# A streaming encoder step: two of eight modulation vectors computed ahead of the SSD, six during the QKV projection, and QKV with weights stationary in chunks of 512 tokens

## The chip, the cores and the metric

One core of one Trainium2 chip. The metric is the device time of one execution in microseconds (us). The core's engines are TensorE (PE, with its weight loads shown apart as PEld), VectorE (DVE), ScalarE (ACT), GpSimd (POOL) and SyncE (SP), which here only issues DMAs. Each engine runs its own instructions in order; semaphores tie them together.

## What is computed

One layer of a hybrid encoder for two request groups: 2048 prompt tokens and 64 sample tokens, model width 1024. The parts that matter here:

```
mod = (silu(c) @ w_ada + b_ada)[:, None, :]              # w_ada (1024, 6144), c: one row per group
sh1, sc1, g1, sh2, sc2, g2 = split(mod, 6)
h = rmsnorm(x, norm1_w) * (1 + sc1) + sh1
m, states = mixer(h, ...)
x = x + g1 * m
h = rmsnorm(x, norm2_w) * (1 + sc2) + sh2
x = x + g2 * hier_moe(h)
...
# mixer:
proj = h @ w_in                                          # w_in (1024, 2832)
z, xbc, dt_raw = proj[..., :i0], proj[..., i0:i1], proj[..., i1:i2]
q, k, v, f_raw = ...                                     # q, k, v: 512 columns each
... conv, SSD scan (Mamba-2) over xbc, dt; forgetting attention over q, k, v, cumsum(log_sigmoid(f_raw + f_bias))
... concatenated @ w_out
# after the layer:
sh_f, sc_f = split(silu(c) @ w_ada_f + b_ada_f, 2)       # w_ada_f (1024, 2048)
y = rmsnorm(y, final_norm_w) * (1 + sc_f) + sh_f
```

The first two modulation vectors (sh1, sc1) are needed by the first norm, the other six only from the output projection on. k and v are returned as well, for both groups.

## The kernel before

All arithmetic is float32. The large products are made of three products of rounded halves (`product3`, lines 265 to 269: high times high, and the two cross terms, of type fp32r); a weight is split by ACT (rounded copy, L255) and DVE (the rest, L260). Small products (modulation, parts of the SSD) are plain float32 matmuls, which the trace shows as two records each.

The program is a row of stages. Each is an `nc.Block()` with one instruction list for each engine; a stage ends with a barrier, so nothing of the next begins before the last DMA of this one has landed. In order:

1. `modulation` (L105). The product with `w_ada` and `w_ada_f` in 16 chunks of 512 columns: `load` two chunks of 2 MB ahead into `wa`, one DMA each (L145, L148); PE multiplies 8 matmuls for each chunk (L187), with 2 columns of `cT` stationary, into `ps`; DVE copies 2 rows out (L212). Then 64 transposes (L198) make columns of them, and biases and `1 +` are applied (L224, L229). In the same block `w_in`'s part for the SSD is loaded and split (`load_split_weights`, L235), through a stage of two slices: slice k waits until slice k-2 is split. DVE does the splits (L260) after its last copy of the modulation. The result also goes to `mod_dram`.
2. `ssd_branch` (L279). For each of the 17 tiles of 128 tokens: norm, `h` (written to HBM as `h_hi`, `h_lo`), projection of z, xbc and dt, conv, SSD.
3. `forget_sums` (L797). The cumulative sums of the log forget values on DVE, and in the same block the load and the split of `w_in`'s q, k and v columns (1536 wide, 8 slices), again through a stage of two slices. DVE splits after the sums.
4. `qkv_projection` (L860). Eight chunks of 256 tokens and one more for the sample tile. A chunk has 8 groups for q and k (128 output columns each; 24 matmuls with the weight stationary and 256 tokens moving), then 2 tiles of v (24 matmuls with `h` stationary and 512 weight columns moving, L267 to L269), then 8 transposes of k (L959). SP stores each chunk's q and k when all 8 groups are split, and loads `h` two chunks ahead (L888). Chunk loops are hardware loops. The cached k rows are loaded, turned and split after the last chunk, two halves one after the other (L929, L974, L1017).
5. Attention, output projection, routing, experts and the final norm, which the diff doesn't touch.

The tensors that the steps below name: `wa` weights of the modulation, `both` the chunk's product, `mod_t` its columns, `b_h_hi`/`b_h_lo` the `h` chunks in SBUF, `wb_hi`/`wb_lo` the q, k, v weights, `b_ps` PSUM banks.

## Time and profile before

| what | us |
|---|---|
| median of 3 runs | 2947.28 (2942.05 to 2951.09) |
| the profiled execution | 2944.57 |
| span of its instructions | 2942.8 |
| PE busy / DVE / ACT / POOL | 2433.4 / 1352.8 / 926.1 / 314.6 |
| modulation stage, from the start to the first instruction of the SSD | 171.6 |
| SSD stage | 171.6 to about 663 |
| forget sums with the weights of QKV | about 663 to 709.8 |
| QKV, first to last matmul of its chunks | 717.4 to 1032.6 |
| first instruction of the attention | 1073.6 |

Times inside the trace count from the span's start. "Busy" of an engine is the time in which an instruction of its own ran. A matmul's duration includes filling and draining the array, and neighbours overlap, so what one costs in a row is the distance between two starts. A row of the timeline says start, duration, engine, line, operation, output and inputs, count, and in brackets how long the engine sat idle before and for whom. For a matmul, 128*2 means 128 rows of contraction and 2 stationary columns; 128x512 is the moving operand. The granted clock of TensorE is given as a share of its upper level of 2.4 GHz; 0.5 is the lower level, 1.2 GHz.

### The profile page before, as it was taken

The numbers are of one execution on the slowest core, as the hardware profiler recorded it, in microseconds if no ns is written. First come the engines' busy times: TensorE is split into PE (matmuls) and PEld (weight loads), VectorE is DVE, ScalarE is ACT, GpSimd is POOL, SyncE is SP. The second block draws the span as 40 slices with busy tenths as digits, with TensorE's granted clock in tenths as the row PEclk, the third lists the DMA queues.
The fourth block names the chain that finished last, engine by engine and source line by source line (L and its number), as shares of the span: only waits on it lengthen the run. The fifth ranks groups of instructions, "written<-read, shape, count | busy, mean of one in ns | idle before, by whom it ended". The sixth has DMA issues, their size and how long they took to land. (4 is left out here: it accounts for less than half of the span.)

```text
span 2942.8 us, 35370 instructions
## 1 busy us (share of the span) xinstructions
PE 2433.4 (83%) x12087; PEld 1874.6 (64%) x12088; DVE 1352.8 (46%) x2648; ACT 926.1 (31%) x1599; POOL 314.6 (11%) x362
## 2 busy tenths in 40 slices
PE   7959999862999918999999489970999999999950
PEld 1248888752999914566555268850788888888840
DVE  0148888863000014555555255653144555235556
ACT  0034444431111112334434333321123443123443
POOL 0000000000000020000000000005122222222220
PEclk9979999975999958999999789985999999999985
DMA  6731112114444352334441244432555777357666
GB/s 230 256 104 68 62 70 75 65 29 146 153 162 157 115 147 57 78 78 88 97 98 37 81 158 142 143 133 77 155 172 171 242 260 267 95 162 230 204 220 253
DMA packets 201131, 407.21 MB, mean 138 GB/s; under 512 B 63930, under 2 KB 85864, under 8 KB 197632
## 3 DMA queue, kind: packets, MB, share of 16 engines
q1 hardware_dynamic: 178624, 329.22, 34.9%
q0 software_dynamic: 20048, 68.37, 9.0%
q10 hardware_dynamic: 2384, 8.65, 0.8%
q8 instruction: 44, 0.72, 0.1%
q14 instruction: 31, 0.25, 0.0%
HBM read 296.12 MB, written 110.07 MB: 138 GB/s over the span
## 5 line engine op out<-in xcount | busy, mean ns | idle before, releaser
L1301 ACT ACTIVATE c_pr<-c_ps,neg_f 128x512 f32<-128x512 f32 (+2 forms) x360 | 195.4, 592 | 362.2 <-PE c_ps L1254 361.2
L1263 PE MATMUL c_po<-c_pr,c_vv 128*66 128x512 f32 (+2 forms) x720 | 276.2, 505 | 0.0
L1325 DVE TENSOR_REDUCE c_mx<-c_pm 128x1 f32<-128x512 f32 (+3 forms) x304 | 178.4, 614 | 195.5 <-PE c_pm L1221 118.5
L1221 PE MATMUL c_pm<-c_km,c_q 66*128 66x512 f32 (+1 forms) x336 | 159.0, 522 | 56.7 <-POOL c_ones_r L1199 27.9
L267 PE MATMUL b_ps<-b_h_hi,wb_hi 128*128 128x256 f32 x576 | 164.6, 286 | 37.7 <-DMA b_h_lo<-h_lo 37.7
L1026 DVE TENSOR_TENSOR b_qk_lo<-b_qk,b_qk_hi 128x2048 fp32r<-128x2048 f32 x11 | 25.2, 2293 | 333.9 <-ACT b_qk_hi L988 333.9
L268 PE MATMUL b_ps<-b_h_lo,wb_hi 128*128 128x256 f32 x576 | 163.7, 284 | 0.0
L269 PE MATMUL b_ps<-b_h_hi,wb_lo 128*128 128x256 f32 x576 | 163.7, 284 | 0.0
L267 PE MATMUL p_zx<-wa_hi,ah_hi 128*128 128x432 f32 x408 | 155.6, 381 | 3.6 <-DVE ah_lo L646 3.6
L267 PE MATMUL x_pg<-x_g_hi,x_x_hi 128*128 128x512 f32 x336 | 136.6, 407 | 23.5 <-DVE x_x_lo L2106 23.5
L1263 PEld LDWEIGHTS c_po<-c_pr,c_vv 128*66 128x66 f32 x720 | 92.4, 139 | 93.2 <-issue 38.3
L268 PE MATMUL p_zx<-wa_lo,ah_hi 128*128 128x432 f32 x408 | 150.2, 368 | 0.0
L269 PE MATMUL p_zx<-wa_hi,ah_lo 128*128 128x432 f32 x408 | 149.5, 366 | 0.0
L267 PE MATMUL x_pd<-x_d_hi,x_m_hi 128*128 128x512 f32 x344 | 140.6, 409 | 6.9 <-DVE x_m_lo L2116 6.9
L268 PE MATMUL x_pd<-x_d_lo,x_m_hi 128*128 128x512 f32 x344 | 136.9, 398 | 0.0
L269 PE MATMUL x_pd<-x_d_hi,x_m_lo 128*128 128x512 f32 x344 | 136.7, 397 | 0.0
L267 PE MATMUL x_pu<-x_u_hi,x_x_hi 128*128 128x512 f32 x336 | 136.6, 407 | 0.0
L1221 PEld LDWEIGHTS c_pm<-c_km,c_q 66*128 66x128 f32 x336 | 63.1, 196 | 115.0 <-DVE c_mx L1325 41.0
L268 PE MATMUL x_pg<-x_g_lo,x_x_hi 128*128 128x512 f32 x336 | 135.8, 404 | 0.0
L269 PE MATMUL x_pg<-x_g_hi,x_x_lo 128*128 128x512 f32 x336 | 135.6, 404 | 0.0
L267 PEld LDWEIGHTS b_ps<-b_h_hi,wb_hi 128*128 128x128 f32 x576 | 111.4, 193 | 37.8 <-DMA b_h_lo<-h_lo 37.8
L1254 PE MATMUL c_ps<-c_q,c_k 97*128 97x512 f32 (+2 forms) x360 | 133.9, 374 | 0.3 <-DVE c_q L1347 0.3
(359 smaller groups left out, 5602.4 us busy)
## 6 DMA issues: line engine op xcount, KB each, us to landing
x_raw_g<-in_w_gate_dram SPq DMA_DIRECT2D x32, 1024.0 KB, 9.3
x_raw_u<-in_w_up_dram SPq DMA_DIRECT2D x32, 1024.0 KB, 14.0
x_raw_d<-in_w_down_dram SPq DMA_DIRECT2D x32, 1024.0 KB, 7.3
wa<-in_w_ada_dram SPq DMA_DIRECT2D x12, 2048.0 KB, 8.0
c_k<-k_hi SPq DMA_DIRECT2D x14, 672.0 KB
h_hi<-ah_hi SPq DMA_DIRECT2D x17, 512.0 KB, 2.6
h_lo<-ah_lo SPq DMA_DIRECT2D x17, 512.0 KB, 3.5
d_mix<-mix SPq DMA_DIRECT2D x17, 512.0 KB
```

Of the source, the lines that this page charges most:

```text
L267: pe.matmul(out, a_hi, b_hi, start=start, stop=False)
L268: pe.matmul(out, a_hi, b_lo, start=False, stop=False)
L269: return pe.matmul(out, a_lo, b_hi, start=False, stop=stop)
L1026: dve.tensor_tensor(qk_lo[:], qk[:], qk_hi[:].bitcast(F32), ALU.subtract).then_inc(lo_ready, 1)
L1221: last = pe.matmul(p_m[x % 2][:, 0:w * P], q2[0:KR, s, u["tile"] * P:(u["tile"] + 1) * P], km[:, s, kc], start=True, stop=not masked)
L1254: pe.matmul(out[:, cols], k2[0:ROW + 1, s, kc], q2[0:ROW + 1, s, qc], start=False, stop=True).then_inc(s_done, 1)
L1263: pe.matmul(p_o[ci % 2][0:VW, cols], vv[:, it["h"] % 2, it["key"], :], pr[:, i % RING, cols], start=it["kb"] == 0, stop=it["last"]).then_i ...
L1301: act.activation(pr[:, n % RING, cols], p_s[n % NPS][:, cols], ACT.Exp, bias=c.neg_f[:, it["h"], it["key"]:it["key"] + 1]).then_inc(exp_do ...
L1325: dve.tensor_reduce(mx[:, u % 2, pc["slot"]:pc["slot"] + 1], src, AX.X, ALU.max).then_inc(mx_done, 1)
```

## The change

- `modulation` computes 4 of 16 chunks (sh1, sc1). The stationary operand is `c.c_pad`, 32 columns of which 2 are not zero, and the eight matmuls of a chunk go to four groups of 32 output partitions in turn (`mod_products`), four matmuls with contraction slices 0 to 3 and four with 4 to 7. DVE copies the full 128x512 bank, and `mod_turn`, 4 matmuls with the 2-column matrix `c.sel` moving, sums the four groups and makes columns. The two first `w_ada` loads are issued ahead of the nine small loads. `mod_dram` is no longer written here.
- The other 12 chunks run inside `qkv_projection`, in halves of 4 matmuls (`first`, `second`) and a `turn`, one such act behind each unit of the projection until all 37 are done. POOL issues their loads, 24 of 1 MB, into two buffers.
- Seven of the eight slices of the q, k, v weights are loaded raw under the SSD (SP, ahead of the first tile's stores); `forget_sums` loads the eighth, splits all (ACT rounds, DVE takes five, POOL three of the rests) and loads the first six tiles of `h`.
- `qkv_projection` works in four chunks of 512 tokens and one of 128 for the sample tile. Every q or k unit is 24 matmuls with 512 tokens moving, in a ring of 3 PSUM banks, and is split and stored by itself through a ring of 4 buffers. v is done tile by tile (17). The four cache tiles of k are units behind the four q units of the first chunk. All loops are unrolled.

```diff
+def mod_products(pe, out, c, w, ks, k0):
+    for k in ks:
+        q = slice(32 * (k % 4), 32 * (k % 4) + 32)
+        last = pe.matmul(out[q, :], c.c_pad[:, k, :], w[:, k - k0, :], start=k < 4, stop=k >= 4)
+def mod_turn(pe, out, c, both):
+    for j in range(4):
+        last = pe.matmul(out[:, 2 * j:2 * j + 2], both[:, j * P:(j + 1) * P], c.sel[:], start=True, stop=True)
 # modulation, SP:
+            for n in range(2):
+                sp.dma_start(wa[:, n], wsrc[:, :, n * CH:(n + 1) * CH]).then_inc(wada_loaded[n], 16)
             for at, src in ((V_BADA, a["b_ada"][0]), ...
-            with sp.Fori(0, 6) as i:
-                for s in range(2):
-                    sp.wait_ge(mod_done, i * 2 + s + 1)
-                    sp.dma_start(wa[:, s], wsrc[:, :, bass.ds((i * 2 + s) * CH, CH)]).then_inc(wada_loaded[s], 16)
-            for n in range(4):
-                sp.wait_ge(mod_done, 13 + n)
-                sp.dma_start(wa[:, n % 2], wfsrc[:, :, n * CH:(n + 1) * CH]).then_inc(wada_loaded[n % 2], 16)
+            for n in range(2, NFIRST):
+                sp.wait_ge(mod_done, n - 1)
+                sp.dma_start(wa[:, n % 2], wsrc[:, :, n * CH:(n + 1) * CH]).then_inc(wada_loaded[n % 2], 16)
             load(sp)
 # modulation, PE:
+            for n in range(NFIRST):
+                pe.wait_ge(wada_loaded[n % 2], 16 * (n // 2 + 1))
+                mod_products(pe, ps[n % 2], c, wa[:, n % 2], range(KD), 0).then_inc(mod_done, 1)
+                pe.wait_ge(mod_copied, n + 1)
+                mod_turn(pe, ps[3], c, both).then_inc(mod_turned, 1)
 # ssd_branch, SP:
             load_x(1)
+            for k in range(EARLY):          # EARLY = 7
+                qkv_weights.load(sp, k, wb_loaded)
             step(0, back=False)
 # forget_sums, SP:
+            for k in range(EARLY, KD):
+                weights.load(sp, k, w_loaded)
             for t in range(PAST // P):
                 sp.dma_start(cl[:, t, :], ...)
-            load(sp)
+            for pair, tile in ((0, 0), (1, 2), (2, 6)):
+                weights.load_h(sp, c, pair, tile, h_loaded)
             sp.wait_ge(lo_ready, 1)
 # qkv_projection:
+    RING, NB = 4, 3
+    acts = [(what, n) for n in range(4, 16) for what in ("first", "second", "turn")] + [("rows", 0)]
+    def program():
+        for n in range(NCH + 1):
+            while u < NU and (units[u]["kind"] == "cache" or units[u]["n"] == n):
+                yield "unit", u
+                if todo:
+                    yield todo.pop(0)
+                u += 1
+            while x < len(tiles) and tiles[x]["n"] == n:
+                yield "v", x
+                if todo:
+                    yield todo.pop(0)
+                yield "k_rows", x
+                x += 1
 # POOL:
+            for n in range(4, 16):
+                for half in range(2):
+                    x = 2 * (n - 4) + half
+                    if x >= 2:
+                        pool.wait_ge(half_done, x - 1)
+                    pool.dma_start(wa[:, half], src[:, 4 * half:4 * half + 4, at * CH:(at + 1) * CH]).then_inc(wada_loaded[half], 16)
 # PE, a unit:
+                if b >= NB:
+                    pe.wait_ge(lo_ready, banked[b - NB] + 1)
+                for k in range(KD):
+                    last = product3(pe, out, w_hi[:, k, cols], weights.lo(k)[:, cols], pick(h_hi, k), pick(h_lo, k), k == 0, k == KD - 1)
```

PE in QKV, before, at the end of a chunk (`b_ps5` is a bank of v, `b_ps6` one of the turned k):

```order
L267 MATMUL b_ps5<-wb_hi,b_h_hi 128x512
L268 MATMUL b_ps5<-wb_lo,b_h_hi 128x512
L269 MATMUL b_ps5<-wb_hi,b_h_lo 128x512
L959 MATMUL b_ps6<-ident,b_qk 128x128 x4
```

PE in QKV, now, in the first chunk behind its last q unit, up to the first k unit (`b_pmod` is the modulation's bank, `b_pk` that of the turned k, `b_pu` that of a unit):

```order
L260 MATMUL b_pu0<-b_h_hi,wb_lo_late 128x512
L112 MATMUL b_pmod<-b_wa,c_pad 32x512 x4
L1068 MATMUL b_pk0<-ident,b_k_rows 128x128 x4
L112 MATMUL b_pmod<-b_wa,c_pad 32x512 x4
L1068 MATMUL b_pk1<-ident,b_k_rows 128x128 x4
L119 MATMUL b_pmod<-sel,b_both 128x2 x4
L1068 MATMUL b_pk0<-ident,b_v 128x128 x4
L112 MATMUL b_pmod<-b_wa,c_pad 32x512 x4
L1068 MATMUL b_pk1<-ident,b_v 128x128 x4
L112 MATMUL b_pmod<-b_wa,c_pad 32x512 x4
L258 MATMUL b_pu1<-b_h_hi,wb_hi 128x512
```

A chunk before was projection alone; now an act of the modulation stands behind every unit, and here, where the units are short cache tiles, the acts follow each other closely.

SP at the start of the SSD, before:

```order
L338 DMA ssm<-in_state_ssm_dram 128x64 x4
L347 DMA x<-in_x_prompt_dram 128x1024
L354 DMA h_hi<-ah_hi 128x1024
L355 DMA h_lo<-ah_lo 128x1024
L347 DMA x<-in_x_prompt_dram 128x1024
```

and now:

```order
L329 DMA ssm<-in_state_ssm_dram 128x64 x4
L338 DMA x<-in_x_prompt_dram 128x1024
L816 DMA wb_raw_early<-in_w_in_dram 128x1536 x7
L345 DMA h_hi<-ah_hi 128x1024
L346 DMA h_lo<-ah_lo 128x1024
L338 DMA x<-in_x_prompt_dram 128x1024
```

The seven weight slices have moved in ahead of the first tile's stores and the third tile's load.

## Rows read from the trace of the kernel before

**Rows 1.** Busy time by stage: us, then each engine, clock, DMA share, GB/s.

```profile
core 0: us, PE busy (x) PEld busy (x) DVE busy (x) ACT busy (x) POOL busy (x), PEclk, DMA share, GB/s
7.50:141.90 134.40, 114.77 (x259) 21.47 (x259) 11.31 (x19) 4.58 (x6) 0.00 (x0) 1.00 0.74 260
141.90:171.60 29.70, 5.75 (x65) 5.37 (x65) 13.30 (x18) 7.71 (x6) 0.00 (x0) 0.54 0.44 136
171.60:661.00 489.40, 422.50 (x2322) 376.08 (x2322) 374.42 (x1180) 213.72 (x413) 38.88 (x34) 0.91 0.18 64
661.00:717.40 56.40, 3.46 (x26) 2.70 (x26) 29.16 (x17) 11.88 (x8) 0.00 (x0) 0.50 0.46 160
717.40:1032.60 315.20, 315.20 (x2232) 297.50 (x2232) 18.34 (x8) 60.91 (x115) 0.00 (x0) 0.99 0.41 143
1032.60:1073.60 41.00, 3.98 (x17) 3.13 (x16) 6.88 (x3) 8.60 (x10) 0.02 (x1) 0.53 0.37 115
```

**Rows 2.** Timeline of the modulation, first chunks: SP, PE.

```profile
7.54 34.03 SPq L145 DMA_DIRECT2D wa<-in_w_ada_dram  x5
...
16.09 16.48 PE L187 MATMUL mod_ps<-wa,cT 128*2 128x512 f32 x32 [4.81 <-DMA wa<-in_w_ada_dram]
...
33.99 13.89 PE L187 MATMUL mod_ps<-wa,cT 128*2 128x512 f32 x32 [1.42 <-DMA wa<-in_w_ada_dram]
```

**Rows 3.** The page's DMA issues: count, KB each, median us to landing.

```profile
wa<-in_w_ada_dram SPq DMA_DIRECT2D x12, 2048.0 KB, 8.0
```

**Rows 4.** Timeline, from the modulation's end to the SSD's first instruction.

```profile
143.26 17.59 SPq L250 DMA_DIRECT2D wa_stage<-in_w_in_dram  x12
...
165.44 1.51 DVE L260 TENSOR_TENSOR wa_lo<-wa_stage,wa_hi 128x1296 fp32r<-128x1296 f32 x1 [1.07 <-ACT wa_hi L255]
...
171.61 0.34 SPq L334 DMA_DIRECT2D x<-in_x_prompt_dram  x1
```

**Rows 5.** Timeline of the SSD: third tile's load, and the instruction that reads it.

```profile
185.22 0.34 SPq L347 DMA_DIRECT2D x<-in_x_prompt_dram  x1
...
206.35 1.05 ACT L510 ACTIVATE junk<-x 128x1024 f32<-128x1024 f32 x1
```

**Rows 6.** Timeline of the forget sums up to QKV: DVE, PE.

```profile
678.83 2.95 DVE L854 TENSOR_TENSOR f_lo<-f_sum,f_hi 8x2688 fp32r<-8x2688 f32 x1
...
707.25 1.76 DVE L260 TENSOR_TENSOR wb_lo<-wb_stage,wb_hi 128x1536 fp32r<-128x1536 f32 x1 [0.87 <-ACT wb_hi L255]
...
717.36 0.58 PE L267 MATMUL b_ps<-b_h_hi,wb_hi 128*128 128x256 f32 x1 [37.69 <-DMA b_h_lo<-h_lo]
```

**Rows 7.** Timeline of PE in QKV, 256 tokens moving: 24 starts apart.

```profile
825.70 0.28 PE L267 MATMUL b_ps<-b_h_hi,wb_hi 128*128 128x256 f32 x1
...
828.58 0.28 PE L267 MATMUL b_ps<-b_h_hi,wb_hi 128*128 128x256 f32 x1
```

**Rows 8.** Timeline of PE, 512 columns moving: 24 starts apart (v); 9 apart (experts).

```profile
851.37 0.39 PE L267 MATMUL b_ps<-wb_hi,b_h_hi 128*128 128x512 f32 x1
...
856.81 0.39 PE L267 MATMUL b_ps<-wb_hi,b_h_hi 128*128 128x512 f32 x1
...
2399.95 0.39 PE L269 MATMUL x_pg<-x_g_hi,x_x_lo 128*128 128x512 f32 x1
...
2402.06 0.40 PE L269 MATMUL x_pg<-x_g_hi,x_x_lo 128*128 128x512 f32 x1
```

**Rows 9.** Timeline of PE in the SSD: float32 matmuls on two halves of the rows.

```profile
268.99 0.37 PE L450 MATMUL p_y<-xbc 64*128 64x128 f32 x1
269.00 0.37 PE L451 MATMUL p_s<-xbc 64*128 64x128 f32 x1
269.20 0.27 PE L450 MATMUL p_y<-xbc 64*128 64x128 f32 x1
```

**Rows 10.** Timeline of PE in the attention: 128 columns moving, three starts apart.

```profile
1187.12 0.28 PE L1251 MATMUL c_ps<-c_neg_ts_r,c_ident_r 128*128 128x128 f32 x1
...
1187.45 0.28 PE L1254 MATMUL c_ps<-c_q,c_k 97*128 97x128 f32 x1
```

More of the change, by code:

```diff
@@ new lines, in qkv_projection @@
+    NU = len(units)
+    banked = [u for u in range(NU) if units[u]["kind"] != "cache"]
+    cached = [u for u in range(NU) if units[u]["kind"] == "cache"]
+    refill = {}
+    for n, pair, tile, count in ((0, 0, 4, 2), (0, 1, 8, 2), (1, 2, 10, 2), (1, 0, 12, 2), (2, 1, 14, 2), (2, 2, 16, 1)):
+        last = max(x for x, t in enumerate(tiles) if t["n"] == n and t["pair"] == pair)
+        refill[last] = (pair, tile, count)
+    arrived = {(0, 0): 0, (0, 1): 0, (1, 2): 0, (1, 0): 1, (2, 1): 1, (2, 2): 1, (3, 0): 2, (3, 1): 2, (4, 2): 2}
@@ L874, in qkv_projection @@
[L874 to L880 removed]
+        w_hi, h_hi, h_lo = weights.hi, weights.h_hi, weights.h_lo
@@ L882, in _, with width, tokens @@
+        def width(u):
+            return 512 if units[u]["kind"] == "cache" else pixel_width(units[u]["n"])
+        def tokens(x):
+            return P if tiles[x]["n"] < NCH else DEC
         @block.sync
         def _(sp):
[L884 to L889 removed]
@@ new lines, in _ @@
+            for what, n in program():
+                if what == "unit":
+                    store_unit(n)
+                elif what == "v":
+                    if n in refill:
+                        pair, tile, count = refill[n]
+                        sp.wait_ge(v_done, n + 1)
+                        weights.load_h(sp, c, pair, tile, h_loaded[pair], count)
+                    store_v(n)
+                elif what == "k_rows":
+                    store_k(n)
+                elif what == "rows":
+                    sp.wait_ge(row_out, 1)
+                    sp.dma_start(c.mod_dram, both[:, 0:P]).then_inc(row_stored, 16)
@@ L962, in _ @@
[L962 to L975 removed]
+            seen = set()
@@ new lines, in times_v, with turn_k @@
+            def times_v(x):
+                t = tiles[x]
+                if x >= 2:
+                    pe.wait_ge(v_out, x - 1)
+                for k in range(KD):
+                    last = product3(pe, p_v[x % 2][:], h_hi[:, t["pair"], t["slot"], k, :], h_lo[:, t["pair"], t["slot"], k, :],
+                                    w_hi[:, k, 8 * P:], weights.lo(k)[:, 8 * P:], k == 0, k == KD - 1)
+                last.then_inc(v_done, 1)
+            def turn_k(x):
+                n = tiles[x]["n"]
+                pe.wait_ge(k32_ready, 4 * n + 4)
+                if x >= 2:
+                    pe.wait_ge(kr_out, x - 1)
+                else:
+                    pe.wait_ge(lo_ready, cached[-1] + 1)
+                at = (tiles[x]["tile"] % 4) * P
+                for j in range(4):
+                    last = pe.transpose(p_k[x % 2][:, j * P:(j + 1) * P], k32[:, j, at:at + P], c.ident[:])
+                last.then_inc(kr_done, 1)
@@ new lines, in _ @@
+            for what, n in program():
+                if what == "unit":
+                    unit(n)
+                elif what == "v":
+                    times_v(n)
+                elif what == "k_rows":
+                    turn_k(n)
+                elif what in ("first", "second"):
+                    half = 0 if what == "first" else 1
+                    pe.wait_ge(wada_loaded[half], 16 * (n - 3))
+                    if half == 0 and n > 4:
+                        pe.wait_ge(mod_biased, n - 4)
+                    mod_products(pe, p_mod, c, wa[:, half], range(4 * half, 4 * half + 4), 4 * half).then_inc(half_done, 1)
+                elif what == "turn":
+                    pe.wait_ge(mod_copied, n - 3)
+                    mod_turn(pe, p_mod, c, both).then_inc(mod_turned, 1)
+                elif what == "rows":
+                    pe.wait_ge(mod_scaled, 4)
+                    pe.transpose(p_mod[:, 0:P], c.mod_t[:].rearrange("p g j -> p (g j)"), c.ident[:]).then_inc(row_T, 1)
```

454 lines of the change are left out of this document (243 added, 211 removed).

## The prediction

> **What bounds the kernel now.** I read the busy time by stage first [rows 1]. Three kinds of stage meet the change. The modulation (7.5 to 141.9) is paced by its loads and its matmuls together: DMA share 0.74, PE busy 114.8 of 134.4 us. The two stretches with PE nearly empty, 141.9 to 171.6 and 661 to 717.4, are loading and splitting of weights, at a DMA share of 0.44 and 0.46: bound by the chain of load, rounding, rest and next load. The chunks of QKV (717.4 to 1032.6) are bound by PE alone, busy all 315.2 us, DMA share 0.41; behind them stand 41.0 us of tail in which PE works 4.0 us. All stages follow each other behind barriers, so what a stage gains, the program gains.
>
> **A. Modulation ahead of the SSD.** 12 of 16 chunks go. Before, 2.1 MB issued at 7.54 fed PE at 16.09 [rows 2], with the median load landing in 8.0 us [rows 3]. Now two loads are issued some 3 us earlier, at about 4.2, and the nine small loads that the first product needs queue behind them. First chunk landed 8.5 us after its issue, the second should need 6.5 more (2.1 MB in the 16.09-7.54-2 us that remain without a start-up of about 2, an estimate), so they are in at 19.5; silu, turn and copy take about 1.5: PE begins at 21. A chunk costs 6.9 us unpacked at full clock (32 records in 13.89 us, two chunks) [rows 2]; packed, at the low clock, I take 3.5 (see D). The third load is issued at 24.5 and lands at 32.5, the fourth behind it at 40.5, its chunk and its turn are done at 47. The first split rest of the SSD's weights is then ready at 48.5. From that point to the last one took 143.26 to 166.95 before [rows 4], 23.7 us, and nothing of that chain changes: 72.2, and 0.7 for the barrier gives 73 instead of 171.6. **-98.5.** If the packing gives nothing, each chunk is 3.5 us longer on a path with three of them: -87.
>
> **B. SSD.** Seven weight slices, 5.5 MB, are put on SP's queue about 7 us into the stage. At 6.5 us for 2.1 MB they end 24 us in. Behind them come the first tile's two stores (1 MB) and the third tile's x; that load was issued at 185.22 and first read at 206.35 [rows 5], that is 34.7 us into the stage. It would land at 24 + 4.6 = 29 to 33: hidden, by a hair. **0**, up to +8 if the queue is slower. What bound this stage (DVE 374 and PE 423 us of 489) is not touched.
>
> **C. Forget sums.** The last matmul-free stretch is 56.4 us [rows 1]. Now two chains run. DVE: the sums ended at 678.83 + 2.95 = 681.8 [rows 6]; their first scan no longer waits for the cache's log values, -3; then five rests instead of eight, 5 x 1.76 = 8.8 [rows 6], and POOL's three beside them, which I let cost DVE up to 3: 688 to 691. DMA: one slice and six tiles of h, 7.1 MB at the rate above, from 666 on: 688 to 691 too. The first matmul then comes at 693 instead of 717.4: **-24**, with -26 and -18 as ends.
>
> **D. QKV, from its first matmul to the attention: 356.2 us before.** Distances between starts: 256 moving, 2.88/24 = 0.120 us [rows 7]; 512 moving, 5.44/24 = 0.2267 in v and 2.11/9 = 0.2344 in the experts [rows 8]; 128 moving with 128 stationary, 0.33/3 = 0.110 [rows 10]. So a 512 wide matmul replaces two of 0.120 for 0.227 to 0.234; I take 0.2306.
> - q and k: 4 x 8 x 24 = 768 by 0.2306 = 177.1 (184.3 before). The sample tile's 192 matmuls: 128 wide instead of 256, 0.110 each, 21.1 (23.0).
> - v: 17 tiles x 24 = 408 by 0.2306 = 94.1 (432 before, one tile of them empty).
> - turned k and cache tiles, 84 transposes by 0.13 = 10.9. Low clock at the start: +1.9, as before.
> - turns, 12 x 4 matmuls of two records by 0.11 (bound by the load of 128 stationary columns, as in [rows 10]) = 10.6.
> - modulation, 24 halves of 4 matmuls. One after another a half costs 3.43 us, if all four run side by side 0.86. The nearest row is a pair on two halves of the rows [rows 9]: both start within 0.01 us, and their second records 0.21 later, so the array does run them side by side. That the step is 0.21 and not 0.11 I read as two loads of 128 stationary columns in a row; here a load is 32 columns. I take 0.86 and an allowance of 0.25 for changing over, 1.11, sum 26.6; bounds 0.86 and 3.5, sums 21 and 84.
> - stalls: 12, from 0 to 25. They come where acts follow closely, the four cache tiles (the listing of PE in QKV, now): a 1 MB half is asked for again after some 4 us and needs 6 to 8. Then the h tiles of chunks 2 and 3, 2 MB with about 14 us of room. Traffic in the first chunk is about 25 MB in 90 us, 280 GB/s, near the 260 of the modulation stage [rows 1]; the rest lies lower.
> - tail: the cache's 31 us (two halves, one after the other) move under the chunks; what is left is copy, store and barrier, 5.
>
> Sum 359.3 against 356.2: **+3**. The 41 us of tail and the wider chunks pay for the modulation, no more.
>
> On the packing, beside the row: the Trainium skill, TensorE: Matmul & The Clock Gate, Part 3 ("Measured speedup vs the span model") gives 2.38 for three column tiles, and TensorEngine Tiling, Overview, up to 4 for four; the pair of [rows 9] shows no gain in total time, the rule would make a half about 1.2 to 1.4 us, an estimate. No run here shows a column tile with a neighbour.
>
> On the 512: the same page, Back-to-back issue gap, gives N/2.4 + 2.5 ns, 109 for 256 and 216 for 512 wide. By it the wider chunk would save 1.5 us, not 7; the trace has 120 and 227, and goes by the load of the weights too.
>
> **Sum.** -98.5 + 0 - 24 + 3 = -119.5 on a span of 2942.8: 2823.3, and 1.8 around it as before: 2825. The profiled run lies 2.7 under the median of the runs, so 2828.
>
> **The rivals.**
> 1. The four column groups do not run side by side in float32. For it: [rows 9] shows no gain in time. Against: the equal starts there. D grows by 24 x 2.4 = 57, less some stalls (6), A by 11: 2890. Half of it (only neighbouring records of two groups overlap, 1.97 a half): 2828 + 20 + 4 = 2852.
> 2. Slower than before: the `w_ada` loads through POOL's queue become the pace of QKV. PE must have each half before it may go on to its next unit, and the ring holds two. The 37 acts take about 226 us of my sum, 18.8 a chunk of 2 MB; the 119.5 us are used up when a chunk takes 28.8 us, that is when a half takes over 25 us from issue to landing. From there on it is slower, with 35 us it would be 3070. Against: 2 MB landed in 8.0 us [rows 3], and QKV left more than half of the DMA time free, share 0.41 [rows 1]. Nothing in the trace shows POOL's queue with such loads, so it keeps a small chance.
> 3. The early weights are not hidden: the stores of `h` come late, and ACT, which may not overwrite `h_hi` before, holds the second tile; PE's clock falls with it. +10 to 15 once: 2840.
> 4. Stalls in QKV are none, and 512 wide goes at 0.2267: 2828 - 12 - 5 = 2811.
>
> **How the numbers follow.** 0.68 for my forecast with its own ends (2805 to 2850; rival 4 is its lower end), 0.10 for half the packing (2852), 0.13 for none (2890), 0.05 for rival 3 (2840), 0.04 for rival 2. The range reaches from 2803, under rival 4, to 2888, which leaves out rival 2, about half of the no-packing case and the tails of mine. A measurement here tells 0.3% (9 us) from no change. All cases but rival 2 are faster by over 0.3%; I give 0.95, 0.01 and 0.04.
>
> **What would show it.** First instruction of the SSD at 73 (A); distance from it to the SSD's last one as before, 489 (B); first QKV matmul 32 us behind that (C); 512 wide starts 0.227 to 0.234 apart, a half of the modulation 1.1 us, and no idle PE over a few us behind `b_wa` or `b_h` loads (D); attention 360 us behind QKV's first matmul. I am wrong if a half costs over 2 us, if PE waits for POOL's loads in every chunk, or if the stage before QKV is held by the six loads of h for much over 30 us.

## The result, and the profile after

The changed kernel takes 2832.35 us (median of four runs, 2827.11 to 2836.92) against 2947.1 for the kernel before in the same session (2942.05 to 2951.09): ratio 0.9611, 95% interval 0.9587 to 0.9635. The forecast was 2828, in a range of 2803 to 2888. Its profiled execution took 2834.98, with a span of 2833.3 where before had 2942.8. That span was forecast at 2823.3, so in the trace the forecast is 10.0 us off, while the medians are only 4 apart: before's profiled run lay 2.7 us under its median, that of the changed kernel 2.6 over its own.

The stages, by the first instruction of each (QKV: its first matmul):

| us | before | changed | difference | forecast |
|---|---|---|---|---|
| A: start of the SSD | 171.6 | 75.5 | -96.1 | -98.5 |
| B: SSD | 492.1 | 495.7 | +3.7 | 0 |
| C: forget sums, up to QKV's first matmul | 53.7 | 34.4 | -19.3 | -24 |
| D: QKV, up to the attention | 356.2 | 355.6 | -0.6 | +3 |
| everything behind | 1869.2 | 1872.1 | +2.9 | 0 |
| span | 2942.8 | 2833.3 | -109.5 | -119.5 |

The busy time by stage answers to [rows 1]; its columns are the same. The first line is now the whole first stage, with the split of the SSD's weights in it; then the SSD, the forget sums, and QKV in four stretches.

```profile
3.20:75.50 72.30, 18.90 (x98) 8.05 (x98) 16.25 (x22) 13.55 (x13) 3.46 (x6) 0.72 0.60 191
75.50:569.00 493.50, 422.07 (x2322) 376.15 (x2322) 373.66 (x1180) 213.47 (x413) 39.19 (x34) 0.91 0.21 75
569.00:607.00 38.00, 4.77 (x28) 3.83 (x29) 32.20 (x14) 11.09 (x8) 16.36 (x5) 0.50 0.56 194
607.00:700.00 93.00, 88.19 (x422) 62.90 (x421) 12.05 (x22) 12.70 (x22) 8.11 (x11) 0.92 0.72 248
700.00:790.00 90.00, 90.00 (x448) 66.85 (x447) 8.42 (x16) 12.71 (x22) 6.73 (x9) 1.00 0.73 258
790.00:880.00 90.00, 90.00 (x431) 70.14 (x430) 10.32 (x22) 12.93 (x23) 2.25 (x3) 1.00 0.53 187
880.00:966.00 86.00, 76.05 (x443) 66.44 (x441) 5.79 (x13) 15.26 (x35) 4.80 (x2) 0.96 0.29 100
```

The first stage has PE busy only 18.9 of 72.3 us. In the forget stage DVE is busy 32.2 of 38, which makes it the bound there. From 700 to 880 PE never rests, at full clock; seven of the twelve chunks of modulation end there, the last at 837.

**Stage A**, timeline (start, duration, engine, line, operation, in brackets the idle time before it), where [rows 2, 4] were:

```profile
4.00 1.04 SPq L158 DMA_DIRECT2D wa<-in_w_ada_dram  x2
...
5.08 8.15 SPq L163 DMA_DIRECT2D vrow<-in_b_ada_dram  x1
...
16.01 0.30 SPq L164 DMA_DIRECT2D vrow<-in_conv_w_dram  x1
23.52 0.31 ACT L182 ACTIVATE srow<-crow 16x128 f32<-16x128 f32 x1 [19.03 <-DMA vrow<-in_conv_w_dram]
...
25.11 3.31 PE L112 MATMUL mod_ps<-wa,c_pad 128*32 128x512 f32 x16 [0.54 <-DVE c_pad L213]
...
49.53 2.92 DVE L251 TENSOR_TENSOR wa_lo<-wa_stage,wa_hi 128x1296 fp32r<-128x1296 f32 x2
```

Issuing one small load behind the two of 2 MB held SP for 8.15 us. The last small load was issued at 16.01 and the silu waited for it until 23.52, where I had all loads in at 19.5. PE's first product came at 25.11 and waited for no weights, since both chunks had landed by 23, 18.7 us behind their issue. The split of the SSD's weights, from 49.53 to the SSD at 75.53, took 26.0 us where I had 24.5.

**Stage C**, timeline of DVE, where [rows 6] were, and that of POOL beside it:

```profile
574.22 4.41 DVE L888 TENSOR_TENSOR_SCAN f_sum<-f_ones,scratch 8x2048 f32<-8x2048 f32 x1
578.66 0.68 DVE L890 COPY f_clt<-f_ps 8x512 f32<-8x512 f32 x1
579.38 3.57 DVE L892 TENSOR_TENSOR_SCAN f_sum<-f_ones,f_clt 8x512 f32<-8x512 f32 x1
582.98 3.46 DVE L894 TENSOR_TENSOR_SCAN f_sum<-f_ones,f_sum,scratch 8x128 f32<-8x128 f32 x1
586.48 4.59 DVE L896 TENSOR_SCALAR f_sum<-f_sum 8x2688 f32<-8x2688 f32 x1
...
595.56 6.75 DVE L877 TENSOR_TENSOR wb_lo_early<-wb_raw_early,wb_hi 128x1536 fp32r<-128x1536 f32 x4
```

```profile
574.22 15.44 POOL L877 TENSOR_TENSOR wb_lo_early<-wb_raw_early,wb_hi 128x1536 fp32r<-128x1536 f32 x3 [19.58 <-ACT wb_hi L873]
```

A scan of 128 columns takes 3.46 us here, almost as long as one of 2048, and the negation 4.59. The next cast of the same size, behind POOL's last rest, took 1.55. The sums end at 595.6, and the first matmul comes at 605.6.

**Stage D**, timeline of PE at the cache tiles (L112 an act of the modulation, four matmuls of two records; L1068 a cache tile):

```profile
634.57 1.06 PE L112 MATMUL b_pmod<-b_wa,c_pad 128*32 128x512 f32 x8
635.56 0.66 PE L1068 MATMUL b_pk<-ident,b_k_rows 128*128 128x128 f32 x4
...
639.14 0.64 PE L1068 MATMUL b_pk<-ident,b_v 128*128 128x128 f32 x4
643.00 1.94 PE L112 MATMUL b_pmod<-b_wa,c_pad 128*32 128x512 f32 x8 [3.22 <-DMA b_wa<-in_w_ada_dram]
644.86 1.12 PE L1068 MATMUL b_pk<-ident,b_v 128*128 128x128 f32 x4
646.47 1.93 PE L112 MATMUL b_pmod<-b_wa,c_pad 128*32 128x512 f32 x8 [0.49 <-DMA b_wa<-in_w_ada_dram]
648.34 0.80 PE L258 MATMUL b_pu<-b_h_hi,wb_hi 128*128 128x512 f32 x1
...
655.91 0.95 PE L119 MATMUL b_pmod<-sel,b_both 128*128 128x2 f32 x8
```

From start to start a half of the modulation costs 0.99 us (634.57 to 635.56), forecast 1.11. Behind the wait of 3.22 us it costs 1.86 (643.00 to 644.86), and the unit from 648.34 to 655.91 takes 7.57, where one at full clock takes 5.58. PE had been idle, and the granted clock was 0.50, its lower level of 1.2 GHz, from 643 to 652 us. In all of QKV PE waited 4.4 us for `w_ada`, in three pieces. The page's DMA issues have POOL's loads at a median of 7.4 us from issue to landing:

```profile
b_wa<-in_w_ada_dram POOLq DMA_DIRECT2D x16, 1024.0 KB, 7.4
```

The 2.9 us behind the attention's start lie in stages that the change doesn't touch. Over the further profiles below, leaving out the kernel without modulation, this part of the program took 1869 to 1873 us, so I take it for its own variation.

### The profile page after: what moved, and what is told of

Read it like the earlier page. It is cut to its first block and busy times, and to the rows that moved or that the text cites. A ratio compares the mean times of both kernels' runs of the same rounds, so it can differ in the third digit from the quotient of the medians.

```text
span 2833.3 us, 33663 instructions
## 1 busy us (share of the span) xinstructions
PE 2359.2 (83%) x11355; PEld 1823.5 (64%) x11356; DVE 1357.9 (48%) x2693; ACT 905.9 (32%) x1574; POOL 345.1 (12%) x389
## 5 line engine op out<-in xcount | busy, mean ns | idle before, releaser
L1426 PEld LDWEIGHTS c_po<-c_pr,c_vv 128*66 128x66 f32 x720 | 92.3, 139 | 92.9 <-issue 38.3
L1176 DVE SCALAR_TENSOR_TENSOR b_lo<-b_pu,b_hi 128x512 fp32r<-128x512 f32 (+1 forms) x40 | 24.5, 612 | 259.3 <-ACT b_hi L1145 259.3
L1411 PE MATMUL c_ps<-c_q,c_k 128*128 128x512 f32 (+2 forms) x360 | 133.4, 372 | 0.0
L260 PE MATMUL x_pu<-x_u_hi,x_x_lo 128*128 128x512 f32 x336 | 133.3, 397 | 0.0
L259 PE MATMUL x_pu<-x_u_lo,x_x_hi 128*128 128x512 f32 x336 | 133.2, 396 | 0.0
L258 PE MATMUL b_pu<-b_h_hi,wb_hi 128*128 128x512 f32 (+1 forms) x320 | 122.3, 382 | 12.1 <-PEq L59 12.1
```

The lines of the kernel that those rows point to most:

```text
L258: pe.matmul(out, a_hi, b_hi, start=start, stop=False)
L259: pe.matmul(out, a_hi, b_lo, start=False, stop=False)
L260: return pe.matmul(out, a_lo, b_hi, start=False, stop=stop)
L1176: dve.scalar_tensor_tensor(out=lo[:, n % RING, 0:w], in0=bank_of(n)[:, 0:w], scalar=HD ** -0.5 if un["kind"] == "q" else 1.0, in1=hi[:, n ...
L1411: pe.matmul(out[:, cols], k1[:, s, kc], q1[:, s, qc], start=True, stop=False)
L1426: pe.matmul(p_o[ci % 2][0:VW, cols], vv[:, it["h"] % 2, it["key"], :], pr[:, i % RING, cols], start=it["kb"] == 0, stop=it["last"]).then_i ...
```

## The experiments

Stage lengths of all kernels in the profiled execution, in us, and the time of each (median of four runs; POOL's rests late has one run). The kernel before had a median of 2948.0 to 2948.5 in these sessions.

| kernel | SSD starts | SSD | forget | QKV | time |
|---|---|---|---|---|---|
| changed | 75.5 | 495.7 | 34.4 | 355.6 | 2832.35 |
| changed, again | 75.2 | 493.6 | 34.4 | 352.6 | 2833.78 |
| one column group | 87.8 | 497.7 | 34.4 | 414.3 | 2906.75 |
| no rests on POOL | 74.9 | 497.5 | 30.5 | 359.6 | 2830.88 |
| POOL's rests late | 74.0 | 497.1 | 35.6 | 354.9 | 2836.72 |
| small loads first | 67.3 | 494.9 | 34.3 | 352.8 | 2824.34 |
| no early weights | 74.3 | 494.4 | 38.3 | 355.2 | 2838.59 |
| no modulation in QKV | 74.4 | 495.2 | 34.3 | 306.6 | (not comparable) |
| no act at the cache tiles | 75.0 | 495.7 | 34.4 | 349.8 | 2829.27 |
| units of 256 | 75.1 | 494.9 | 34.3 | 361.1 | 2843.09 |
| three edits | 67.7 | 496.2 | 30.4 | 346.5 | 2811.08 |
| three edits, deep stage | 56.9 | 495.0 | 30.4 | 346.4 | 2801.24 |

**1. The changed kernel again.** No edit.

> The changed kernel again, unaltered, in one session with the others: a second profile tells how far a stage's length moves by itself. Over six profiles with the changed kernel's SSD, the stage took 494 to 498 us, against 492 in the one of before; without the early loads it took 494. Theory (the 3.7 us that the SSD became longer is mostly how this stage varies): it comes out between 493 and 499 with its steps at other tiles. The other stages should be within 1 us of the first profile, QKV 354 to 357 with the wait at the cache tiles, the time 2829 to 2835.

Measured: 2833.78 (2830.80 to 2836.83), ratio 0.9617 (0.9601 to 0.9633). The SSD took 493.6, 2.1 us less than in the first profile. QKV took 352.6, a little under what I expected: the wait at the cache tiles was there (3.34 us), but the clock was back at full 3.4 us behind its end, so that the second act and the unit behind it took 1.00 and 5.57 us instead of 1.86 and 7.57. So a single profile settles the length of the SSD or of QKV only to 2 or 3 us, and smaller differences of these two are not read. The forget stage came out at 34.3 to 34.4 in every version that leaves it alone.

**2. Is it the packing that makes the modulation cheap?**

```diff
-        q = slice(32 * (k % 4), 32 * (k % 4) + 32)
-        last = pe.matmul(out[q, :], c.c_pad[:, k, :], w[:, k - k0, :], start=k < 4, stop=k >= 4)
+        last = pe.matmul(out[0:32, :], c.c_pad[:, k, :], w[:, k - k0, :], start=k == 0, stop=k == 7)
```

> The changed kernel, but all eight products of a modulation chunk go to the first group of 32 columns and add up there, instead of four groups side by side. Theory (the four groups run side by side: four matmuls took 1.00 us in QKV): without it a half costs 4 x 0.86 = 3.43 us, so the 24 halves in QKV cost 24 x 2.43 = 58 us more, less a little where PE waited for loads anyway (4.4 us in all); ahead of the SSD, where chunk, turn and next load are in a row, +3.5 us for each of four chunks, 10 to 14. In all +66 to +72 over the changed kernel's 2832, so 2900. Rival (the groups only look short because the profiler closes their records early, and the array did the same work before): no row gets longer and the time stays within 3 us of 2832. Second rival (the loads set the pace of the modulation, not PE): the first stage stays as it is, and only QKV grows.

DVE then copies 32 rows instead of 128, into a `both` that is zeroed once. Measured: 2906.75, ratio 0.9858 (0.9841 to 0.9874), 74.4 us over the changed kernel, a little more than expected. QKV grew by 58.7, the SSD started 12.3 later. Timeline of PE, a half in QKV with its neighbour, and a chunk of the first stage:

```profile
698.76 3.62 PE L111 MATMUL b_pmod<-b_wa,c_pad 128*32 128x512 f32 x8
702.31 0.50 PE L259 MATMUL b_pu<-b_h_hi,wb_hi 128*128 128x512 f32 x1
...
44.28 7.05 PE L111 MATMUL mod_ps<-wa,c_pad 128*32 128x512 f32 x16
```

From start to start a half now costs 3.55 us instead of 0.99: a factor of 3.6 for four groups side by side. The Trainium skill, TensorEngine Tiling, Overview, gives up to 4, and TensorE: Matmul & The Clock Gate, Part 3 ("Measured speedup vs the span model"), 2.38 for three; here the larger is nearly reached. The prediction's estimate from 2.38, a half of 1.2 to 1.4 us, was too long: a half costs 0.99, or 1.2 with the changing over that experiment 7 finds. Both rivals fall: the rows did get longer, and the first stage grew too.

**3. Does POOL help in the forget stage?**

```diff
-        POOL_KS = (1, 4, 6)
+        POOL_KS = ()
```

> The changed kernel, but DVE takes all eight rests in the stage of the forget sums, POOL none. In the changed kernel POOL's three rests took 5.1 us each, and beside them DVE's scan of 2048 took as before only in part: a 512 wide scan 3.57 us (1.19 before the change), the last scan 3.46 (0.47), the negation 4.59 (1.55). Theory (POOL and DVE hold each other up, and POOL's help costs more than it gives): the sums end at about 15 us into the stage instead of 24, eight rests of 1.7 follow, 13.6, and QKV's first matmul comes 30 to 31 us into the stage instead of 34.4: -4 us. Rival (DVE was slow for another reason, such as the DMA traffic of the h tiles): the sums stay as they are and three more rests come on top, +5 us. Second rival: the loads of h are the bound at 34 us, no change.

Measured: 2830.88, ratio 0.96 (0.9584 to 0.9616). The forget stage fell to 30.5, as expected. Timeline of its DVE:

```profile
580.52 1.21 DVE L892 TENSOR_TENSOR_SCAN f_sum<-f_ones,f_clt 8x512 f32<-8x512 f32 x1
581.77 0.47 DVE L894 TENSOR_TENSOR_SCAN f_sum<-f_ones,f_sum,scratch 8x128 f32<-8x128 f32 x1
582.28 1.55 DVE L896 TENSOR_SCALAR f_sum<-f_sum 8x2688 f32<-8x2688 f32 x1
```

The three instructions take 3.2 us instead of 11.6. Eight rests instead of five cost 5.0 of these 8.4 again; 3.4 are left, and the stage became 3.9 shorter. In the time little of it arrived: in this profile QKV took 359.6, 4.0 more than in the first profile of the changed kernel, with waits for `w_ada` of 2.8, 3.2 and 2.0 us. That profile was also of the slowest of the kernel's four runs (2837.52), so how much was given back is open to 2 or 3 us.

**4. What does the hindering look like from the other side?**

```diff
+            pool.wait_ge(lo_ready, 1)
             for k in POOL_KS:
                 take_lo(pool, k)
```

> The changed kernel, but POOL begins its three rests when DVE's sums are done (it waits for the last of them). Theory (the two hold each other up, instruction beside instruction): the sums end 15 us into the stage as without POOL, instead of 24; then DVE's five rests take more than the 1.7 each that they took alone, 3 or more beside a rest of POOL, and POOL's three end last, 15 + 15.4 = 30 us into it; the first matmul at 34 to 36. Rival (DVE was slow for another reason): DVE's sums still end at 24.

Measured: forget stage 35.6, 2836.72 in one run. DVE's rests in the timeline, then POOL's line by itself, here and in the changed kernel (its columns: durations in ns, least, median and most; first and last start):

```profile
587.00 6.75 DVE L877 TENSOR_TENSOR wb_lo_early<-wb_raw_early,wb_hi 128x1536 fp32r<-128x1536 f32 x4
593.68 1.74 DVE L877 TENSOR_TENSOR wb_lo_late<-wb_raw_late,wb_hi 128x1536 fp32r<-128x1536 f32 x1
```

```profile
L877 POOL TENSOR_TENSOR wb_lo_early<-wb_raw_early,wb_hi x3: 3408/3409/11546, 587.2 to 602.0; 128x1536 fp32r<-128x1536 f32 x3
```

```profile
L877 POOL TENSOR_TENSOR wb_lo_early<-wb_raw_early,wb_hi x3: 3529/4328/7648, 574.2 to 586.1; 128x1536 fp32r<-128x1536 f32 x3
```

The sums went at full speed, as expected, but one part of the theory was wrong: DVE's rests were not slowed, 1.69 each as alone. POOL's first rest took 11.5 us and the other two 3.41. It began at 587.15 and ended at 598.7, which is 3.3 behind the end of DVE's last rest at 595.4. So the two don't share, one stands while the other works: POOL waited out all five rests of DVE, which follow each other without a gap. The changed kernel's own rows fit this to 0.2 us. POOL's rests took 7.65, 4.33 and 3.53 there, and ended at 581.9, 586.2 and 589.7. DVE's three slow instructions ended at 582.95, 586.44 and 591.07, which is 1.1, 0.3 and 1.4 later, about what each takes alone (1.21, 0.47, 1.55). DVE's copy out of PSUM at 578.66 took the 0.68 us that it takes in the kernel before, with a rest of POOL running, so not every instruction of DVE is held. The Trainium skill says it of the same pair (SBUF — State Buffer, "SBUF: two separate sides"): the port pair of DVE and GpSimd is an exclusive lock, held for a whole instruction, by DVE for one with two SBUF inputs or in a 2-port mode. By that rule, the trace agrees. A rest costs 3.4 us of the pair on POOL and 1.7 on DVE, so handing one over loses wherever DVE needs the pair too.

**5. The small loads first.**

```diff
-            for n in range(2):
-                sp.dma_start(wa[:, n], ...).then_inc(wada_loaded[n], 16)
             for at, src in ((V_BADA, a["b_ada"][0]), ...
             sp.dma_start(vrow[V_CW:V_CB, :], ...
+            for n in range(2):
+                sp.dma_start(wa[:, n], ...).then_inc(wada_loaded[n], 16)
```

> The changed kernel, but in the first stage the nine small loads (biases, norms, convolution) are issued ahead of the two 2 MB loads of w_ada. In the changed kernel the issue of the first small load behind them held SP for 8.15 us, the last small load was issued at 16.0, the silu came at 23.5 and the first product at 25.1 us. Theory (the queue is full behind the two large loads, and that wait is on the path): the first product comes when the first 2 MB are in, about 4.2 + 4 + 8.5 = 17 us, the SSD starts 6 to 8 us earlier, at 68 to 69. Rival (the transfers of w_ada are the path, and moving them back by the 4 us of nine issues costs what it gives): SSD start at 73 to 76, no change.

Measured: 2824.34, ratio 0.9583 (0.9567 to 0.9599), 8.0 us under the changed kernel. Timeline:

```profile
4.00 0.32 SPq L161 DMA_DIRECT2D vrow<-in_b_ada_dram  x1
...
7.21 1.03 SPq L164 DMA_DIRECT2D wa<-in_w_ada_dram  x2
10.74 0.31 ACT L182 ACTIVATE srow<-crow 16x128 f32<-16x128 f32 x1 [6.26 <-DMA vrow<-in_conv_w_dram]
...
16.58 3.64 PE L112 MATMUL mod_ps<-wa,c_pad 128*32 128x512 f32 x16 [4.79 <-DMA wa<-in_w_ada_dram]
```

The same issue takes 0.32 us instead of 8.15, PE begins at 16.58 and now waits for its weights, and the SSD starts 8.2 earlier. The small loads had been on the path. The rival's price did not come either: the two large loads, issued 3.2 us later, were in by 22, a little earlier than before. Busy time while they move, in the changed kernel, here, and in the kernel before (columns as in [rows 1]; the last is GB/s):

```profile
5.00:22.50 17.50, 0.00 (x0) 0.00 (x0) 0.00 (x0) 0.00 (x0) 2.20 (x5) 1.00 0.86 244
```

```profile
11.00:21.00 10.00, 4.32 (x18) 1.03 (x18) 1.06 (x3) 1.75 (x4) 0.00 (x0) 1.00 1.04 391
```

```profile
11.00:19.00 8.00, 3.19 (x5) 0.48 (x5) 0.37 (x2) 1.26 (x3) 0.00 (x0) 1.00 1.05 392
```

With the large loads first, the DMA moved 244 GB/s where it otherwise moved over 390. Why stays open.

**6. No early weights.**

```diff
 # ssd_branch, SP:
-            for k in range(EARLY):
-                qkv_weights.load(sp, k, wb_loaded)
 # forget_sums, SP:
-            for k in range(EARLY, KD):
+            for k in range(KD):
```

> The changed kernel without the early loads: the seven slices of QKV's weights (5.5 MB) are loaded in the stage of the forget sums, ahead of everything there, and none under the SSD. Theory (the early loads are hidden under the SSD and take time from nothing there; the 3.7 us that the SSD became longer began with the first x load, which is issued ahead of them, and with single tiles late in the stage): the SSD keeps its 495 us give or take 2, and the forget stage moves 13.4 MB at 0.32 MB/us instead of 7.9, +13 to +17 us on its 34.4. In all 2845 to 2849. Rival (the early loads are what lengthened the SSD by 3.7): the SSD returns to 492, and the gain of loading early is smaller, 2842 to 2845.

Each slice has a semaphore of its own here. Measured: 2838.59, ratio 0.9634 (0.9618 to 0.965), 6.2 over the changed kernel. The SSD took 494.4, inside the 493.6 to 497.7 of the kernels with the early loads, so no cost of them on the SSD is seen. The forget stage grew by 3.9 only. First the DMA view of 568 to 612 in 40 slices, then the timeline of DVE:

```profile
GB/s 0 89 318 408 436 425 408 419 447 425 408 424 436 419 408 347 370 413 410 413 410 398 406 413 413 413 410 413 410 400 103 0 0 0 0 7 34 311 408 417
```

```profile
588.22 0.68 DVE L886 COPY f_clt<-f_ps 8x512 f32<-8x512 f32 x1 [12.21 <-PE f_ps L858]
...
596.91 6.75 DVE L873 TENSOR_TENSOR wb_lo_early<-wb_raw_early,wb_hi 128x1536 fp32r<-128x1536 f32 x4
```

The queue moves over 400 GB/s in most slices, 413 on average from 571 to 590 us, not the 323 that I had worked out from the landing of the first chunk. The trace of the kernel before had shown it: its line in experiment 5 has 392. This is a good part of why holding the weights back costs so little. What it did cost came by another way than I expected: the cache's log values queue behind the weights, and DVE waits 12.2 us for them. POOL does its rests in that gap, so almost nothing is hindered (DVE's scan of 128 is back at 0.47 us).

**7. No modulation in QKV.** The twelve chunks under QKV are left out, with their loads, and their vectors stand at zero.

```diff
-    acts = [(what, n) for n in range(4, 16) for what in ("first", "second", "turn")] + [("rows", 0)]
+    acts = [("rows", 0)]
```

> The changed kernel with no modulation in QKV: the twelve chunks under QKV are left out altogether (loads, products, turns, copies; the six modulation vectors stand at zero, so later values differ, not the work). It measures what the modulation costs QKV. By my terms that was 24 halves at 1.00 us (24), 12 turns at 0.81 (9.7), waits for loads 4.4 and the low clock behind the wait in the cache tiles, about 6: QKV goes from 355.6 us to 311 to 314. If the acts cost only their own matmuls and the wait and low clock come from elsewhere (the stage's start, the cache tiles' own short transposes), it goes to 318 to 322. If the modulation's loads slow the h loads and stores too, to below 308.

Measured: QKV 306.6, less than I expected. With the modulation at zero the experts stage has more work (1053.6 us instead of 827.6), so nothing behind QKV is compared, nor the time. All of the modulation costs QKV 46.0 us against the repeated profile and 49.0 against the first. In the first profile the acts' matmuls, from start to start, are 24 x 0.99 + 12 x 0.81 = 33.5, and the waits for `w_ada` 4.4. The low clock behind them costs 0.9 for each of two acts, 0.5 for a cache tile and 2.0 for a unit, 4.3. That leaves 6.8. Some 6 of it are in the timeline of a version whose acts lie between units:

```profile
622.37 0.39 PE L260 MATMUL b_pu<-b_h_hi,wb_lo_late 128*128 128x512 f32 x1
622.68 1.06 PE L112 MATMUL b_pmod<-b_wa,c_pad 128*32 128x512 f32 x8
623.68 0.50 PE L258 MATMUL b_pu<-b_h_hi,wb_hi 128*128 128x512 f32 x1
624.02 0.39 PE L259 MATMUL b_pu<-b_h_lo,wb_hi 128*128 128x512 f32 x1
```

the act starts 0.31 behind the last matmul of a unit instead of 0.23, and the unit's second start lies 0.34 behind its first instead of 0.23. So changing over costs 0.2 for a half. A turn costs 0.1: it starts at the usual distance, and only the unit's second start behind it is late (656.72 to 657.04 in the changed kernel). 24 x 0.2 + 12 x 0.1 = 6.0.

The rest is the low clock at the start of QKV: from first to last matmul the first unit took 8.15 us in the first profile, 6.85 in the repeated one and 6.75 here. So the first profile adds up to 33.5 + 4.4 + 4.3 + 6.0 + 1.4 = 49.6 for 49.0, and the repeated one, with 5.6 of waits and 1.4 of low clock behind them, to 33.5 + 5.6 + 1.4 + 6.0 + 0.1 = 46.6 for 46.0. The 306.6 lies where I expected it if the loads of `w_ada` slowed those of `h` too. No such cost is in the rows: PE waits for no `h` within QKV, in either version.

**8. No act at the cache tiles.**

```diff
                 yield "unit", u
-                if todo:
+                if todo and units[u]["kind"] != "cache":
                     yield todo.pop(0)
```

> The changed kernel, but no act of the modulation stands behind the four cache tiles; those acts come behind later units. In the changed kernel PE waited there for a load of w_ada 3.2 us at 643.0, in two other versions 3.2 and 3.4 at the same place, and the granted clock fell to its lower level for the act, its turn and the unit behind (act 1.94 us instead of 1.07, unit 7.57 instead of 5.6). Theory (the acts follow each other there in under 4 us each, the load needs 7, and the wait brings the clock down): no wait over 1 us behind the first, QKV 346 to 349 us instead of 355.6, the time 6 to 9 us under the changed kernel. Rival (the cache tiles' transposes alone let the clock fall, and the loads have to be waited for wherever the acts stand): QKV stays at 353 to 356.

Measured: QKV 349.8, 2829.27, ratio 0.9592 (0.9576 to 0.9608). The wait for `w_ada` at the cache tiles and the low clock behind it are gone, so the acts' closeness made them, and not the transposes. Another wait stayed, at the very first act, where the changed kernel had waited 0.67 us and, repeated, 1.88:

```profile
614.45 1.31 PE L112 MATMUL b_pmod<-b_wa,c_pad 128*32 128x512 f32 x8 [2.15 <-DMA b_wa<-in_w_ada_dram]
615.69 0.80 PE L258 MATMUL b_pu<-b_h_hi,wb_hi 128*128 128x512 f32 x1
```

and behind it the clock fell again (0.80 and not 0.50 for the unit's first matmul, 7.00 us instead of 5.67 for the unit). QKV therefore fell by 3 to 6 us, not by 7 to 10, and the time by 3.

**9. Units of 256.**

```diff
-                for k in range(KD):
-                    last = product3(pe, out, w_hi[:, k, cols], ..., pick(h_hi, k), pick(h_lo, k), ...)
+                for i in range(len(pairs)):
+                    for k in range(KD):
+                        last = product3(pe, out[:, i], w_hi[:, k, cols], ..., h_hi[:, pairs[i], :, k, :], h_lo[:, pairs[i], :, k, :], ...)
```

> The changed kernel with each 512 wide matmul of q and k of the four full chunks split into two of 256, all eight slices for the first half, then for the second: 768 matmuls become 1536, everything else stays. By the spacings of the trace (256 wide 0.120 us, 512 wide 0.2325 in these units) the split costs 768 x (0.240 - 0.2325) = 6 us, QKV 361 to 362. By 0.109 and 0.216, the gap of a few ns that the Trainium skill gives (TensorE: Matmul & The Clock Gate, Back-to-back issue gap), it would cost 1.5 us. Rival: the second half stalls, or spreads the loads' waits differently, and it changes by less than 3 us either way.

Measured: QKV 361.1, 5.5 and 8.5 over the two profiles of the changed kernel; 2843.09, ratio 0.9647 (0.9631 to 0.9663), 10.7 over its time. Here too the clock came back one act sooner, as in the repeated profile, so 8.5 is the better comparison. A unit takes 5.86 us up to the turn behind it, instead of 5.58, and 32 x 0.28 = 9.0. The expectation had 6, since it took 0.2325 for a 512 wide matmul, which has the changing over in it; units in a row have 0.227. The 1.5 us are not borne out that the Trainium skill (TensorE: Matmul & The Clock Gate, Back-to-back issue gap) would give, by a formula that it states for a single matmul alone. What sets the pace is argued and not shown: 128 columns moving take 0.110 us [rows 10] and 256 take 0.120, each with its own load of 128 stationary columns, so the load seems to bound both.

**10. Three edits together**: those of 3, 5 and 8, and no act behind the very first unit.

```diff
-                if todo:
+                if todo and u > 0 and units[u]["kind"] != "cache":
```

> The changed kernel with three edits together: the small loads ahead of the first w_ada loads, no rests on POOL, and no act of the modulation behind the very first unit or behind the cache tiles. With POOL's rests alone taken away the forget stage became 3.9 us shorter, but QKV 4.0 longer, with longer waits for w_ada (2.8 at the first act, 3.2 and 2.0 at the cache tiles). Theory (what ended that gain was the waits for w_ada and the low clock behind them, which this version hasn't): SSD start 67 to 68, forget stage 30.5, QKV 345 to 348, and the time 20 us under the changed kernel's 2832, so 2812. Rival (a stage that starts earlier only waits longer in QKV, whatever the order of the acts): QKV 353 or more, the time 2818 or more.

Measured: 2811.08, ratio 0.9539 (0.9523 to 0.9555): SSD start 67.7, forget 30.4, QKV 346.5, and PE never waits for `w_ada` there. With the waits gone, POOL's 4 us arrive in the time. By stages the edits are worth 8, 4 and 6 to 9 us, 18 to 21 together; in the time they are 21.

**11. And a deeper stage for the SSD's weights**, four slices instead of two.

```diff
-                sp.wait_ge(split, k - 1)
+                sp.wait_ge(split, k - D + 1)          # D = 4, slice k % D
```

> As the kernel of three edits, and the stage through which the SSD's weights are loaded holds four slices instead of two. With two slices the eight rests stood 41.4 to 66.5 us in the profile with the small loads first, 25 us for 8 x 1.51 of work, each pair behind a load that was issued when the slice two before had been split. Theory (that chain of load, rounding, rest is what paces the stretch): slices 4 to 7 land while the first four are split, the stretch shrinks by 8 to 11 us, SSD start at 57 to 60. Rival (the DMA is full there with the w_ada loads, or the loads of more slices take DMA from w_ada and make the modulation later): SSD start at 64 to 67.

Measured: 2801.24, ratio 0.9501 (0.9485 to 0.9517), 9.8 under the one without and 31 under the changed kernel. Timeline of DVE in the first stage:

```profile
41.08 5.75 DVE L252 TENSOR_TENSOR wa_lo<-wa_stage,wa_hi 128x1296 fp32r<-128x1296 f32 x4
...
52.94 3.15 DVE L252 TENSOR_TENSOR wa_lo<-wa_stage,wa_hi 128x1296 fp32r<-128x1296 f32 x2 [0.24 <-ACT wa_hi L247]
```

Four rests follow each other, and the eight take 15.0 us (41.08 to 56.1) instead of 25. This is the fastest version of the study.

## Why the prediction was right, and where its steps were off

**The frame held.** Stages behind barriers, each with its own bound, so that their differences add up: forecast -119.5, measured -109.5, and every term has its sign or lies within 3.7 us of zero. That 2828 came within 4 us of the median is in part luck. The stages' errors are +2.4, +3.7, +4.7, -3.6 and, behind the attention's start, +2.9; only one of them has the other sign, and 5 us of their 10 were made up by where the two profiled runs lay among their runs. The repeated profile has a span of 2828.3, 5 us over the forecast. Rivals 1 and 2 are out: the four groups run side by side (experiment 2), and a 1 MB half landed in 7.4 us (median), not in over 25. Half of the packing, 1.97 us a half, is out with rival 1. Rival 3 did not come either: the early loads cost nothing that can be told from the SSD's variation (6).

**A, -98.5 against -96.1.** That the nine small loads queue behind the two large ones stood in the prediction, but the term for it was mis-sized: both large loads in at 19.2 and silu at 19.5, in truth about 23 and 23.5, with the DMA at 244 GB/s instead of over 390 (5). SP stood 8.15 us on one issue, but that need not be the cause: the last small load was issued by 16.3, with the large ones still moving. So the first product came at 25.1, not 21. Part of it came back: the fourth load landed 9.7 us behind its issue at 32.2, which is 5.4 behind the third instead of 8, and PE didn't wait for it. The last turn was done at 49.1, not 47, and the first rest came at 49.5 instead of 48.5. The split from there to the SSD took 1.5 us longer. The forecast took the order of the loads as given and didn't ask what it costs: 8 us (5). And it said that nothing of the split's chain changes, which held; but that chain was worth 10 us to anyone who would change it (11).

The term for no packing was -87, 11.5 less; measured 12.3 less.

**B, 0 against +3.7.** Eleven profiles with the early loads gave 493.6 to 497.7, and the one without them 494.4. The kernel before has 492.1 in its one profile. Whether something in the changed kernel makes the SSD 2 us longer, or whether that one profile was short, stays open. In the first profile 1.9 of the 3.7 us were there before the second tile: ACT waited 4.24 us for the first x instead of 2.38, and that load is issued ahead of the early weights. The step itself, that the third tile's x lands before it is read, held: its load went out 15.5 us into the stage and the SSD's steps went on at their old distance.

**C, -24 against -19.3: the step that failed.** "POOL's three beside them, which I let cost DVE up to 3": they cost 8.4 us, and DVE's own three rests would have cost 5.0. Without POOL the term is -23.2, the forecast's (3, 4). The second chain, DMA, was mis-sized the other way. I took 0.32 MB/us from the first chunk's landing less an estimated start-up of 2 us; the rows of that same trace have 392 GB/s once the loads run (5), and the forget stage without early weights 413 (6). So that chain was done some 14 us before DVE's.

**D, +3 against -0.6.** Term by term: a half 0.99 instead of 1.11 from start to start, plus 0.2 for changing over, which is 1.19, so 28.6 instead of 26.6; turns 0.81 instead of 0.88, with their changeover 0.9, so 10.9 instead of 10.6. Stalls were 12 in the forecast, and 4.4 of waits and 4.3 of low clock in the trace. The whole modulation under QKV was 49.2 in the sum (26.6 + 10.6 + 12) and 46 to 49 on the chip (7), the halves too cheap and the stalls too dear. The place was the forecast's too, the cache tiles, and experiment 8 shows it. The wider matmuls were forecast at 7 us and gave 9 (9): 512 wide went at 0.227 in units in a row, as in rival 4, and not at 0.2306. A unit of the sample tile was forecast at 21.1 for all eight; they took 21.5.

Not foreseen was that the clock ties these together: behind the wait of 3.2 us the low clock cost another 4.3 in the first profile, and 1.4 behind one of 3.3 in the repeated one.

## What to carry to other kernels

Before work is handed to POOL beside DVE, look at what kinds of instructions stand on both sides: where both need the port pair their times add up, and POOL held it twice as long as DVE for the same work. Done while DVE waited, POOL's rests hindered almost nothing (6); whether they pay beside instructions of DVE that leave the pair alone was not tried. Put the small loads that the first result needs ahead of the large ones on a queue, and give a load-round-split chain more than two buffers when its DMA share is at a half. Spread side work by the time that its loads need: the waits of over 2 us here were paid twice, once as idle and once as low clock.

## What the runs showed of the hardware

- Four float32 matmuls with 32 stationary columns each, in four column groups, 512 moving: 0.99 us side by side, 3.55 in one group.
- DVE and POOL shut each other out for whole instructions, where DVE's was a scan, a rest or the negation; a copy out of PSUM was not held. A 128-column scan of 0.47 us took 3.46, and a rest of 3.41 us on POOL took 11.5 beside five of DVE.
- Issuing a small DMA behind two of 2 MB held SP for 8.15 us; ahead of them it took 0.32.
- Plain loads from one queue moved 413 GB/s over 19 us in the forget stage (6) and 392 over 8 us in the modulation before, whose mean with its pauses is 260 [rows 1].
- The same two loads of 2 MB moved at 244 GB/s when issued ahead of nine small ones, and at 391 behind them (5).
- After PE's wait of 3.2 us the granted clock was at the lower level until 9 us behind the wait's end, in the repeated profile until 3.4 us behind it: an act took 1.94 instead of 1.06, a unit 7.57 instead of 5.58. Waits of 0.67 and 1.88 us at the first act of QKV were followed by acts at full clock (1.07 and 1.06).
